# A gated-delta stage of a two-block kernel: loads, sums, masks and block turns reordered across its queues

## The chip, the cores and the metric

One core of one Trainium2 chip. The metric is the device time of the whole program in microseconds (us), median of several runs.

## What is computed

The program runs two model blocks on a 512-token latent and a 256-token context of width 2048. The change lies in one stage of the first block, the gated-delta mixer (8 heads of width 128, two directions). Per head, with 6 chunks of 128 tokens:

```python
q = l2_norm(qkv[:, :, 0]) * (K ** -0.5); k = l2_norm(qkv[:, :, 1]); v = qkv[:, :, 2]
gcum = jnp.cumsum(g, axis=-1)
decay = jnp.exp(jnp.where(incl, gcum[..., :, None] - gcum[..., None, :], -jnp.inf))
a_strict = jnp.where(strict, jnp.einsum('bhcik,bhcjk->bhcij', k_beta, k) * decay, 0.0)
sol = lax.linalg.triangular_solve(a_strict, rhs, left_side=True, lower=True, unit_diagonal=True)
attn = jnp.einsum('bhcik,bhcjk->bhcij', q, k) * decay
q_dec = q * jnp.exp(gcum)[..., None]
def step(S, inp):
    qd, ke, ui, wi, ai, dec = inp
    v_new = ui - jnp.einsum('bhqk,bhkv->bhqv', wi, S)
    o = jnp.einsum('bhqk,bhkv->bhqv', qd, S) + jnp.einsum('bhqs,bhsv->bhqv', ai, v_new)
    return S * dec[..., None, None] + jnp.einsum('bhsk,bhsv->bhkv', ke, v_new), o
```

The first output normalisation, the output projection and the second block follow in other stages.

## The kernel before, in words

The stage is `gdn_stage`. Each engine has its own list of instructions, written out by hand, and waits on semaphores; the order within an engine's list is fixed. Heads are worked in four pairs (`PAIRS`, j = 0 to 3). In the opening, heads 0 to 3 are prepared, and 8 output columns of the output projection of the other mixer half (`mix`, matmuls of L2356 to L2358) run on TensorE beside VectorE's triangle of pair 0. Then the loop over pairs; `more` means that there is a next pair, `ahead` that there is one after it (true for j = 0 and 1), whose heads are a+2, b+2 in the lists (a, b inside `steps`).

Work of a pair, in the order of TensorE: `level5_t` (L476) needs the spread inverse blocks (`scatter_in`, the SyncE loads of L319); `turn_k(a)`, `level5_x` (L490), `level5_y` (L501), `q_sums` of the heads ahead (L414), `turn_k(b)`, `level6_t` (L509), `finish(j - 1)` (L607), `level6_y` (L520), `turn_v`, `weights` (L538), `k_sums` of the heads ahead (L405, L406), then `steps(j)`. In `steps`, six steps n = 0 to 5, each for two directions: L565, L570 and, after ScalarE's scaled copy `v_end` (L784), L578, which VectorE turns into the new state (L1091 for n = 0, L1095 after); from n = 2 on L598 and L599 write the outputs. Between the steps of pairs 0 and 1 stand the products of the heads ahead: `queries` (L451) and `products` (L461).

ScalarE takes the squares of q and k (`square_q` L696, `square_k` L688), logarithm and inverse root (`ln_*`, `inverse_*` L715, L711), the evacuations, the exponentials of the decay (`decay`, L732, 12 small ones a head) and of q's scale (`queries`, L738), `turn_tri` (L742), and the norm of the pair before (`norm_ln` L838, `norm_exp` L842). VectorE scales k (`keys`, L1030), evacuates (`level5_x`, L1053), solves the 32-wide triangles of the next pair (`triangle`, L1043 and L1046, 31 of them, `TRI_EARLY` of them ahead of `steps`), ends the pair before (`finish`, L1111, L1113), normalises q (`norm_q`, L1005) and k (L1000), makes `attention` (L1010), `decayed` (L1017) and `turned` (L1024). GpSimd adds the mask to the decay's argument (`argument`, L952), multiplies q with its scale (`queries`, L957), writes the identity (`identity`, L964) and issues stores. SyncE issues the loads; `gather` (L287, 8 transfers a head) writes the Gram parts to memory, `blocks_load` (L294) reads them back as 32-wide blocks, `scatter_out` (L299) and `scatter_in` (L319) move the solved blocks.

## Time and profile before

| What | us |
|---|---|
| Median of 3 runs (3778.26 to 3779.26) | 3778.9 |
| The profiled execution | 3775.26 |
| its span, first to last instruction | 3773.5 |
| the gated-delta stage in it, 972 to 1384 us | 412 |

Mean granted clock of TensorE is 0.975 over the span. Times in the rows below are us from the start of the span; a line of a timeline has start, duration, engine, source line, and in brackets how long the engine was idle before it and who ended that.

### The profile page before, as it was taken

What the parts mean: (1) busy time and instruction counts of PE and PEld (TensorE: products, weight loads), DVE (VectorE), ACT (ScalarE), POOL (GpSimd) and SP (SyncE); (2) the same over time, 40 slices, a digit from 0 to 9 for tenths busy, and PEclk for the clock granted to TensorE, in tenths of its full rate; (3) what the DMA queues carried; (4) which work ended last, traced back from release to release, by engine and by line L of the source; (5) the groups of instructions that cost most, each with busy time, mean ns of one, the idle gap of its engine ahead of it and who ended that gap; (6) DMA issues with size and microseconds to landing.
All of it is one profiled execution on the core that took longest, in us unless ns stands there. A gap on an engine that the chain in (4) does not pass through costs nothing. (4 is left out here: it accounts for less than half of the span.)

```text
span 3773.5 us, 49646 instructions
## 1 busy us (share of the span) xinstructions
PE 3565.7 (94%) x19794; PEld 2959.4 (78%) x19794; DVE 1966.6 (52%) x2979; ACT 1510.6 (40%) x2532; POOL 471.2 (12%) x362
## 2 busy tenths in 40 slices
PE   6999999899776789999999999999999999999998
PEld 4688888787655668888888788888888888888886
DVE  7455555467566634755455553436533444454543
ACT  3322222254644443565565642324222444442332
POOL 1000000134211000011011160120000000025021
PEclk8999999999988899999999999999999999999999
DMA  9734323332533336422223163335634555543332
GB/s 360 260 131 137 114 95 103 96 98 59 180 107 92 97 119 195 126 84 87 86 74 93 54 201 98 95 90 103 132 115 124 123 94 111 111 128 101 93 95 89
DMA packets 580503, 448.37 MB, mean 119 GB/s; under 512 B 64454, under 2 KB 500114, under 8 KB 579504
## 3 DMA queue, kind: packets, MB, share of 16 engines
q1 hardware_dynamic: 572080, 421.18, 39.6%
q10 hardware_dynamic: 6048, 19.14, 1.3%
q0 software_dynamic: 2144, 4.87, 0.4%
q8 instruction: 157, 2.57, 0.3%
q14 instruction: 74, 0.61, 0.1%
HBM read 387.61 MB, written 57.46 MB: 118 GB/s over the span
## 5 line engine op out<-in xcount | busy, mean ns | idle before, releaser
L2379 DVE TENSOR_TENSOR w_lo<-w,w_hi 128x512 fp32r<-128x512 f32 x429 | 291.3, 698 | 500.1 <-ACT w_hi L2372 499.9
L2372 ACT ACTIVATE w_hi<-w 128x512 fp32r<-128x512 f32 x429 | 260.9, 625 | 478.0 <-PE od_acc L2358 171.1
L4511 DVE TENSOR_TENSOR w_lo<-w,w_hi 128x512 fp32r<-128x512 f32 x260 | 232.2, 899 | 353.6 <-ACT w_hi L4404 352.2
L4370 PE MATMUL ta_acc<-u_hi,w_hi 128*128 128x512 f32 x960 | 375.2, 391 | 2.8 <-POOL u_lo L4305 1.4
L4372 PE MATMUL ta_acc<-u_hi,w_lo 128*128 128x512 f32 x960 | 373.6, 389 | 0.0
L4371 PE MATMUL ta_acc<-u_lo,w_hi 128*128 128x512 f32 x960 | 373.5, 389 | 0.0
L4404 ACT ACTIVATE w_hi<-w 128x512 fp32r<-128x512 f32 x260 | 163.5, 630 | 440.8 <-PE ta_acc L4372 433.9
L2356 PE MATMUL od_acc<-u_hi,w_hi 128*128 128x512 f32 x768 | 304.7, 397 | 0.0
L2358 PE MATMUL od_acc<-u_hi,w_lo 128*128 128x512 f32 x768 | 299.3, 390 | 0.0
L2357 PE MATMUL od_acc<-u_lo,w_hi 128*128 128x512 f32 x768 | 299.0, 389 | 0.0
L2356 PE MATMUL ev_acc<-u_hi,w_hi 128*128 128x512 f32 x608 | 250.3, 412 | 14.7 <-DVE w_lo L2379 5.1
L2358 PE MATMUL ev_acc<-u_hi,w_lo 128*128 128x512 f32 x608 | 238.8, 393 | 0.0
L2357 PE MATMUL ev_acc<-u_lo,w_hi 128*128 128x512 f32 x608 | 238.7, 393 | 0.0
L1941 PE MATMUL p_acc<-u_hi,p_w_hi 128*128 128x512 f32 x544 | 215.8, 397 | 2.9 <-DVE p_w_lo L1749 2.5
L1948 PE MATMUL p_acc<-u_hi,p_w_lo 128*128 128x512 f32 x544 | 216.0, 397 | 0.0
L4370 PEld LDWEIGHTS ta_acc<-u_hi,w_hi 128*128 128x128 f32 x960 | 180.2, 188 | 43.7 <-DVE u_lo L4519 3.1
L1942 PE MATMUL p_acc<-u_lo,p_w_hi 128*128 128x512 f32 x544 | 212.2, 390 | 0.0
L4372 PEld LDWEIGHTS ta_acc<-u_hi,w_lo 128*128 128x128 f32 x960 | 180.2, 188 | 37.6
L4371 PEld LDWEIGHTS ta_acc<-u_lo,w_hi 128*128 128x128 f32 x960 | 180.2, 188 | 37.5 <-issue 0.5
L2085 DVE TENSOR_TENSOR p_w_lo<-p_w,p_w_hi 128x1024 fp32r<-128x1024 f32 x66 | 80.4, 1223 | 225.1 <-ACT p_w_hi L1987 225.1
L1987 ACT ACTIVATE p_w_hi<-p_w 128x1024 fp32r<-128x1024 f32 x66 | 69.6, 1060 | 247.9 <-PE p_acc L1948 178.0
L2357 PEld LDWEIGHTS od_acc<-u_lo,w_hi 128*128 128x128 f32 x768 | 144.3, 188 | 31.0 <-issue 1.9
(754 smaller groups left out, 8062.4 us busy)
## 6 DMA issues: line engine op xcount, KB each, us to landing
w<-in_o_w_in_dram SPq DMA_DIRECT2D x260, 256.0 KB, 6.6
w<-in_e_w_in_dram SPq DMA_DIRECT2D x144, 256.0 KB, 2.9
p_w<-in_w_in_dram SPq DMA_DIRECT2D x70, 512.0 KB, 6.2
mod_w<-in_w_ada_dram SPq DMA_DIRECT2D x32, 1024.0 KB, 11.8
w<-in_ple_gate_w_dram SPq DMA_DIRECT2D x128, 256.0 KB, 2.7
gate_w<-in_w_ada_dram SPq DMA_DIRECT2D x16, 1024.0 KB, 5.7
z_w<-in_w_in_dram SPq DMA_DIRECT2D x64, 256.0 KB, 2.9
w<-in_e_w_out_dram SPq DMA_DIRECT2D x64, 256.0 KB, 2.7
```

The source lines that it names most:

```text
L1941: pe.matmul(lat, wh, x_hi[:, k, :], start=first, stop=False)
L1942: pe.matmul(lat, wh, x_lo[:, k, :], start=False, stop=False)
L1948: last = pe.matmul(lat, wl, x_hi[:, k, :], start=False, stop=end)
L2356: pe.matmul(out, hi, self.x_hi[:, k, :], start=first, stop=False)
L2357: pe.matmul(out, hi, self.x_lo[:, k, :], start=False, stop=False)
L2358: last = pe.matmul(out, lo, self.x_hi[:, k, :], start=False, stop=end)
L2372: act.activation(self.w_hi[m % self.ring][:], self.w[m % self.ring][:], ACT.Copy).then_inc(self.hi_set, 1)
L2379: eng.tensor_tensor(self.w_lo[m % self.ring][:], self.w[m % self.ring][:], self.w_hi[m % self.ring][:].bitcast(F32), ALU.subtract).then_in ...
L4370: pe.matmul(bank, hi, hi_x[:, k, :], start=(k == 0), stop=False)
L4371: pe.matmul(bank, hi, lo_x[:, k, :], start=False, stop=False)
L4372: last = pe.matmul(bank, lo, hi_x[:, k, :], start=False, stop=(k == job.kd - 1))
L4511: dve.tensor_tensor(self.w_lo[m % RING][:], self.w[m % RING][:], self.w_hi[m % RING][:].bitcast(F32), ALU.subtract).then_inc(self.lo_set, 1)
```

## The change

Nothing of the arithmetic changes; instructions are moved.

- GpSimd's eight mask additions (`argument`) and eight q scalings (`queries`) become VectorE's: in the opening for heads 0 to 3 and 0 to 1, in the loop the scalings after the early triangles, the mask additions in step 0 of `steps`.
- `TRI_EARLY` goes from 14 to 18, ten instead of six triangle steps stand ahead of `finish`.
- SyncE: `scatter_in(0)` ahead of `gather(2)`; `load_q` of the heads ahead goes in front of `blocks_load`.
- TensorE: `q_sums` after `level6_t`; `finish` after `turn_v(a)`; `k_sums` from ahead of `steps` to its step n = 1; `queries` and `products` one step later, the last part after `steps`.
- ScalarE: squares and logarithm of q, `norm_ln`, `norm_exp` later, squares of k ahead of the scalings' exponentials, decay exponentials a step later, `turn_tri` at n = 3 instead of 4.
- VectorE: norms of k, `attention`, `decayed`, `turned` half a step to a step later; `decayed(b, 1)` after the steps.

```diff
--- before.py
+++ after.py
@@ -203,7 +203,7 @@
         S_STEPS = 2 * (CHUNKS - 1)
         O_STEPS = 2 * LC
         TRI_STEPS = B32 - 1
-        TRI_EARLY = 14
+        TRI_EARLY = 18
         MIX_SOLVED = 56
 
         def by_job(upto, eng, step):
@@ -343,8 +343,8 @@
                 load_v(hd)
             mix.load_weights(sp, len(mix.chunks))
             scatter_out(0)
+            scatter_in(0)
             gather(2)
-            scatter_in(0)
             gather(3)
             sp.wait_ge(mix.chunk_done, len(mix.chunks))
             mix.wait_stored(sp)
@@ -352,13 +352,13 @@
             for j in range(PAIRS):
                 more, ahead = j + 1 < PAIRS, j + 2 < PAIRS
                 a, b = 2 * j + 4, 2 * j + 5
+                if ahead:
+                    load_q(a)
+                    load_q(b)
                 if more:
                     blocks_load(j + 1)
                 if not more:
                     tail.load_weights(sp, len(tail.chunks))
-                if ahead:
-                    load_q(a)
-                    load_q(b)
                 if more:
                     load_qdec(2 * j + 2)
                     load_qdec(2 * j + 3)
@@ -547,16 +547,17 @@
                 pe.wait_ge(k_copied, 4 * (j + 1))
                 for n in range(CHUNKS):
                     if ahead:
-                        if n == 2:
+                        if n == 1:
+                            k_sums(a)
+                            k_sums(b)
+                        if n == 3:
                             queries(a)
                             products(a, range(0, 4))
-                        if n == 3:
+                        if n == 4:
                             products(a, range(4, CHUNKS))
-                        if n == 4:
+                        if n == 5:
                             queries(b)
                             products(b, range(0, 4))
-                        if n == 5:
-                            products(b, range(4, CHUNKS))
                     if not more and n in (2, 4):
                         tail.pe_steps(pe, TAIL)
                     for d in range(2):
@@ -641,31 +642,30 @@
                     tail.pe_steps(pe, TAIL)
                 level5_x(j)
                 level5_y(j)
-                if ahead:
-                    q_sums(a + 2)
-                    q_sums(b + 2)
                 if more:
                     turn_k(b)
                 else:
                     tail.pe_steps(pe, TAIL)
                 level6_t(j, 0)
                 level6_t(j, 1)
-                if j > 0:
-                    finish(j - 1)
+                if ahead:
+                    q_sums(a + 2)
+                    q_sums(b + 2)
                 level6_y(j, 0)
                 level6_y(j, 1)
                 if more:
                     turn_v(a)
                 else:
                     tail.pe_steps(pe, TAIL)
+                if j > 0:
+                    finish(j - 1)
                 weights(j, 0)
                 if more:
                     turn_v(b)
                 weights(j, 1)
+                steps(j)
                 if ahead:
-                    k_sums(a + 2)
-                    k_sums(b + 2)
-                steps(j)
+                    products(b + 2, range(4, CHUNKS))
                 if more and not ahead:
                     pe.wait_ge(v_copied, 2 * GDN_H)
                     pe.wait_ge(k_copied, 2 * GDN_H)
@@ -792,11 +792,10 @@
                         if n == 0:
                             ln_k(a)
                             inverse_k(a)
-                            decay(a, range(0, 3))
                         if n == 1:
                             ln_k(b)
                             inverse_k(b)
-                            decay(a, range(3, 6))
+                            decay(a, range(0, 2))
                     for d in range(2):
                         c = ORDER[d][n]
                         if 2 <= n < 4:
@@ -810,10 +809,10 @@
                                            ACT.Copy).then_inc(o_set, 1)
                     if ahead:
                         if n == 2:
-                            decay(b, range(0, 3))
-                        if n == 3:
-                            decay(b, range(3, 6))
-                    if j + 1 < PAIRS and n == 4:
+                            decay(a, range(2, 6))
+                        if n == 4:
+                            decay(b, range(0, 6))
+                    if j + 1 < PAIRS and n == 3:
                         turn_tri(j + 1)
                     if j == PAIRS - 2 and n >= 2:
                         k = n - 2
@@ -900,21 +899,19 @@
                     copy_k(a)
                 else:
                     tail_job(2)
-                if ahead:
-                    square_q(a + 2)
-                    square_q(b + 2)
                 level5_y(j)
                 if more:
                     copy_k(b)
                 else:
                     tail_job(3)
                 if ahead:
+                    square_q(a + 2)
+                    square_q(b + 2)
+                level6_t(j, 0)
+                level6_t(j, 1)
+                if ahead:
                     ln_q(a + 2)
                     ln_q(b + 2)
-                level6_t(j, 0)
-                level6_t(j, 1)
-                if j > 0:
-                    norm_ln(j - 1)
                 level6_y(j, 0)
                 level6_y(j, 1)
                 if more:
@@ -922,20 +919,22 @@
                 else:
                     tail_job(4)
                 if j > 0:
-                    norm_exp(j - 1)
+                    norm_ln(j - 1)
                 weights(j, 0)
                 if more:
                     copy_v(b)
+                if j > 0:
+                    norm_exp(j - 1)
                 weights(j, 1)
                 if ahead:
-                    inverse_q(a + 2)
-                    inverse_q(b + 2)
+                    square_k(a + 2)
+                    square_k(b + 2)
                 if more:
                     queries(a)
                     queries(b)
                 if ahead:
-                    square_k(a + 2)
-                    square_k(b + 2)
+                    inverse_q(a + 2)
+                    inverse_q(b + 2)
                 steps(j)
                 square(j)
                 if more and not ahead:
@@ -947,16 +946,6 @@
 
         @block.gpsimd
         def _(pool):
-            def argument(hd):
-                pool.wait_ge(arg_in[hd % 4], 16 * (hd // 4 + 1))
-                pool.tensor_tensor(a_t[hd % 4][:], a_t[hd % 4][:], neg[:].unsqueeze(1).to_broadcast([P, CHUNKS, 2, P]), ALU.add).then_inc(dec_arg, 1)
-
-            def queries(hd):
-                pool.wait_ge(q_normed, hd + 1)
-                pool.wait_ge(qdec_exp, hd + 1)
-                pool.tensor_tensor(qdec[hd % 4][:], qdec[hd % 4][:], q_n[hd % 4].rearrange("p (c q) -> p c q", c=LC).unsqueeze(2)
-                                   .to_broadcast([P, LC, 2, P]), ALU.mult).then_inc(q_decayed, 1)
-
             def identity(j):
                 if j > 0:
                     for n in range(2):
@@ -965,21 +954,12 @@
                 pool.wait_ge(tri_init, 2 * j + 1)
                 pool.memset(tri[:].rearrange("p i j -> p (i j)")[:, 0:B32 * B32:B32 + 1], 1.0).then_inc(tri_init, 1)
 
-            for hd in range(4):
-                argument(hd)
             identity(0)
-            queries(0)
-            queries(1)
             for n in range(MIX_JOBS):
                 mix.store(pool, n)
             for j in range(PAIRS):
                 if j + 1 < PAIRS:
                     identity(j + 1)
-                    queries(2 * j + 2)
-                    queries(2 * j + 3)
-                if j + 2 < PAIRS:
-                    argument(2 * j + 4)
-                    argument(2 * j + 5)
             for n in range(len(tail.jobs)):
                 tail.store(pool, n)
 
@@ -1003,6 +983,16 @@
                 dve.wait_ge(q_inv, hd + 1)
                 dve.wait_ge(q_squared, hd + 1)
                 dve.tensor_tensor(q_n[hd % 4], q_n[hd % 4], sq_q[hd % 2][:], ALU.mult).then_inc(q_normed, 1)
+
+            def argument(hd):
+                dve.wait_ge(arg_in[hd % 4], 16 * (hd // 4 + 1))
+                dve.tensor_tensor(a_t[hd % 4][:], a_t[hd % 4][:], neg[:].unsqueeze(1).to_broadcast([P, CHUNKS, 2, P]), ALU.add).then_inc(dec_arg, 1)
+
+            def queries(hd):
+                dve.wait_ge(q_normed, hd + 1)
+                dve.wait_ge(qdec_exp, hd + 1)
+                dve.tensor_tensor(qdec[hd % 4][:], qdec[hd % 4][:], q_n[hd % 4].rearrange("p (c q) -> p c q", c=LC).unsqueeze(2)
+                                  .to_broadcast([P, LC, 2, P]), ALU.mult).then_inc(q_decayed, 1)
 
             def attention(hd):
                 dve.wait_ge(dec_set, hd + 1)
@@ -1066,20 +1056,26 @@
                                     triangle(j + 1, at)
                                     at += 1
                             if ahead and slot == 1:
+                                if n == 0 and d == 0:
+                                    argument(a)
                                 if n == 0 and d == 1:
+                                    argument(b)
+                                if n == 1 and d == 1:
                                     norm_k(a)
-                                if n == 1 and d == 1:
+                                if n == 2 and d == 0:
                                     norm_k(b)
-                                if n == 2 and d == 1:
+                                if n == 3 and d == 0:
                                     attention(a)
-                                if n == 3:
-                                    decayed(a, d)
+                                if n == 3 and d == 1:
+                                    decayed(a, 0)
                                 if n == 4 and d == 0:
+                                    decayed(a, 1)
+                                if n == 4 and d == 1:
                                     turned(a)
-                                if n == 4 and d == 1:
+                                if n == 5 and d == 0:
                                     attention(b)
-                                if n == 5:
-                                    decayed(b, d)
+                                if n == 5 and d == 1:
+                                    decayed(b, 0)
                             if slot == 0 and n < CHUNKS - 1:
                                 dve.wait_ge(s_ready, S_STEPS * j + 2 * n + d + 1)
                                 if n >= 2:
@@ -1102,6 +1098,7 @@
                             dve.tensor_tensor(o[:, :, cols], o[:, :, cols], bank[6 + d][:, 0:256].rearrange("p (h q) -> p h q", h=2),
                                               ALU.add).then_inc(o_set, 1)
                 if ahead:
+                    decayed(b, 1)
                     turned(b)
 
             def finish(j):
@@ -1118,6 +1115,8 @@
                     dve.tensor_tensor(y_lo[:, k, :], y_lo[:, k, :].bitcast(F32), y_hi[:, k, :].bitcast(F32), ALU.subtract
                                       ).then_inc(mix.x_set, 1)
 
+            for hd in range(2):
+                argument(hd)
             for hd in range(2):
                 norm_k(hd)
             for hd in range(2):
@@ -1131,6 +1130,10 @@
             mix.split_low(dve, 1)
             split_y(range(2, MIX))
             mix.split_low(dve, mix.ring)
+            for hd in range(2, 4):
+                argument(hd)
+            for hd in range(2):
+                queries(hd)
             for n in range(TRI_STEPS):
                 triangle(0, n)
                 if n in (7, 9):
@@ -1157,14 +1160,17 @@
                     dve.memset(y_by_d[1][:], 0.0).then_inc(cleared, 1)
                 if not more:
                     tail.split_low(dve, 6)
-                for n in range(6 if more else 0):
+                for n in range(10 if more else 0):
                     triangle(j + 1, n)
                 if j > 0:
                     finish(j - 1)
                 if not more:
                     tail.split_low(dve, len(tail.chunks))
-                for n in range(6, TRI_EARLY if more else 0):
+                for n in range(10, TRI_EARLY if more else 0):
                     triangle(j + 1, n)
+                if more:
+                    queries(2 * j + 2)
+                    queries(2 * j + 3)
                 if ahead:
                     norm_q(2 * j + 4)
                     norm_q(2 * j + 5)
```

## Rows read from the trace of the kernel before

**Rows 1.** Stretches of the stage: us, busy of each engine, TensorE's granted clock, transfers

```profile
972.00:1073.40 101.40, 77.23 (x372) 61.12 (x372) 78.71 (x119) 57.60 (x121) 27.39 (x18) 0.89 0.57 176
1073.40:1156.85 83.45, 57.13 (x701) 50.02 (x701) 48.61 (x106) 42.22 (x99) 12.83 (x6) 0.82 0.34 92
1156.85:1247.10 90.25, 60.25 (x705) 51.20 (x705) 55.06 (x108) 44.34 (x102) 13.15 (x6) 0.81 0.33 91
1247.10:1317.60 70.50, 53.87 (x680) 47.34 (x680) 46.81 (x106) 33.28 (x73) 5.41 (x3) 0.86 0.41 106
```

**Rows 2.** Waits from 970 to 1384 us: who waited for whom, us, times, longest

```profile
PE gdn_bank L570 <- DVE gdn_state L1091: 17.5, 3, 6.9
...
PE gdn_bank L414 <- ACT kq L696: 12.9, 2, 7.0
...
PE gdn_bank L405 <- ACT gdn_sq_k L688: 12.9, 5, 4.5
```

**Rows 3.** Stretches, same columns (PE, PEld, DVE, ACT, POOL): triangles alone, then beside GpSimd

```profile
1085.50:1095.80 10.30, 8.21 (x115) 5.96 (x116) 9.25 (x28) 7.40 (x16) 0.00 (x0) 0.80 0.63 216
...
1190.40:1202.60 12.20, 7.06 (x28) 4.76 (x28) 12.06 (x5) 7.01 (x16) 12.04 (x4) 0.85 0.20 76
1269.60:1274.60 5.00, 1.85 (x14) 1.48 (x12) 4.93 (x3) 1.89 (x5) 4.83 (x2) 1.00 0.95 289
```

**Rows 4.** Groups of instructions, GpSimd, 970 to 1384 us: count, busy us, mean ns, idle before

```profile
L952 POOL TENSOR_TENSOR gdn_a_t<-gdn_a_t,k_neg 128x1536 f32<-128x1536 f32 x8 | 29.6, 3724 | 41.7 <-DMA gdn_a_t<-s_cum_rows 41.7
L957 POOL TENSOR_TENSOR gdn_qdec<-gdn_qdec,kq 128x1024 f32<-128x1024 f32 x4 | 10.2, 2568 | 68.8 <-ACT gdn_qdec L738 68.8
```

**Rows 5.** Groups of instructions, VectorE, 1050 to 1390 us

```profile
L1030 DVE TENSOR_TENSOR gdn_w_neg<-gdn_k_tok,gdn_tabs 128x1536 f32<-128x1536 f32 x8 | 13.6, 1736 | 0.0
...
L1010 DVE TENSOR_TENSOR gdn_attn<-gdn_bank,gdn_a_t 128x1024 f32<-128x1024 f32 x6 | 7.3, 1210 | 0.0
...
L1005 DVE TENSOR_TENSOR kq<-kq,gdn_sq_q 128x512 f32<-128x512 f32 x1 | 0.7, 692 | 0.0
```

**Rows 6.** Timeline of pair 0, from the last weights to the gather of the fifth head

```profile
1101.70 0.60 ACT L771 ACTIVATE gdn_w_neg<-gdn_bank 128x512 f32<-128x512 f32 x1 [0.30 <-PE gdn_bank L538]
...
1105.31 1.56 ACT L688 ACTIVATE gdn_sq_k<-kq 128x768 f32<-128x768 f32 x2
...
1112.64 0.49 DVE L1091 COPY gdn_state<-gdn_bank 128x128 f32<-128x128 f32 x2 [7.62 <-PE gdn_bank L578]
...
1113.05 3.57 DVE L1043 TENSOR_TENSOR gdn_part<-gdn_blk,gdn_tri 96x256 f32<-96x256 f32 x1
...
1132.65 0.71 PE L461 MATMUL gdn_bank<-kq 128*128 128x128 f32 x4 [3.20 <-DVE gdn_attn L1010]
...
1147.89 2.12 SPq L287 DMA_DIRECT2D s_blocks_in<-gdn_a_t  x4
```

**Rows 7.** Timeline of pair 1, from its first product to its first state copy

```profile
1156.85 1.02 PE L476 MATMUL gdn_bank<-gdn_x_m,gdn_a_t 32*32 32x32 f32 x96 [3.34 <-DMA gdn_x_m<-s_blocks_out]
...
1168.61 0.20 DVE L1043 TENSOR_TENSOR gdn_part<-gdn_blk,gdn_tri 96x31 f32<-96x31 f32 x1 [4.56 <-DMA gdn_blk<-s_blocks_in]
...
1183.93 0.69 DVE L1111 TENSOR_TENSOR gdn_o<-gdn_o,gdn_o_sq 128x512 f32<-128x512 f32 x1 [11.85 <-ACT gdn_o_sq L842]
...
1205.71 0.49 DVE L1091 COPY gdn_state<-gdn_bank 128x128 f32<-128x128 f32 x2
```

**Rows 8.** Timeline of the opening: norms, then the moves of solved blocks

```profile
993.18 2.05 PE L451 MATMUL gdn_bank<-kq 128*128 128x128 f32 x8 [8.34 <-DVE kq L1005]
...
1064.40 2.12 SPq L287 DMA_DIRECT2D s_blocks_in<-gdn_a_t  x4
...
1073.44 1.50 PE L476 MATMUL gdn_bank<-gdn_x_m,gdn_a_t 32*32 32x32 f32 x96 [7.11 <-issue]
```

**Rows 9.** Timeline of pair 2: first triangle step, first state copy

```profile
1258.08 0.20 DVE L1043 TENSOR_TENSOR gdn_part<-gdn_blk,gdn_tri 96x31 f32<-96x31 f32 x1 [4.70 <-DMA gdn_blk<-s_blocks_in]
...
1278.78 0.49 DVE L1091 COPY gdn_state<-gdn_bank 128x128 f32<-128x128 f32 x2
```

## The prediction

> **What bounds the kernel now.** I read the stretches first. In the four of the gated-delta stage TensorE is busy for 57 to 60 of 83 to 90 us in pairs 0 and 1, 54 of 70.5 in pair 2, and the granted clock falls to 0.81 to 0.89 [rows 1]. No engine fills its time: the stage is a chain that goes from engine to engine, and what counts is which wait ends last at each hand-over. The table of waits names three of TensorE's: for the first state copy of VectorE (17.5 us in 3), for the squares of q (12.9 in 2) and for the squares of k (12.9 in 5) [rows 2]. Then I asked why VectorE is late with the first state copy. In the third view, 14 triangle steps (28 instructions) take 10.3 us when GpSimd is idle. From 1190.4 to 1202.6 VectorE finishes five instructions in 12.06 busy us while GpSimd is busy for 12.04; in pair 2 three take 4.93 beside GpSimd's 4.83 [rows 3]. In pair 0 a triangle product takes 3.57 us beside GpSimd's mask addition [rows 6]. A GpSimd operation here takes 3.7 us (mask) or 2.6 us (q scaling) [rows 4], and each VectorE instruction that meets one lasts until it is over. So the stall is in front of the state copy, on the path.
>
> **The parts and their prices**, as time gained up to fixed points: the first state copy of each pair (L1091), and the first product of the next (L476).
>
> *GpSimd's 16 operations to VectorE.* The nearest rows in VectorE are 1.74 us for two operands of 128x1536 in SBUF, one broadcast, and 1.21 us for a 128x1024 product [rows 5]. Eight and eight make 23.5 us of new VectorE work. What it removes: in pair 1 12.06 us for five instructions that alone take 0.37 each (10.3 over 28), 10.2 us; in pair 2 4.93 less 1.1, 3.8 us; in pair 0 3.57 less 0.4, 3.2 us [rows 3, 6]. The bounds of one moved mask addition are 1.2 and 3.7 us, I take 1.74, the same shape.
>
> *Opening and pair 0 up to its state copy.* TensorE's 8.34 us for the norms shrink [rows 8], but ScalarE then waits in its own list for a load and comes about as before; I keep 3.5 us at the end of the mix. Solved blocks issued ahead of `gather(2)` come 2.1 to 4.3 us earlier (a gather is two lines of 2.12) [rows 8], but the third and fourth head's Gram parts that much later, so the triangles of pair 1 start about 1 us later. The terms: last weight evacuation at 1102.3 [rows 6]; it comes 3 us earlier, since squares of q, fetched ahead of the blocks, no longer stand before the fifth level: 1099.3. Behind it ScalarE has squares of k, exponentials and inverse roots, 4.6 us (1102.3 to 1106.87) [rows 6], say 5.0: 1104.3. VectorE: two q norms at 0.69 [rows 5] and one triangle of 0.9: state copy at 1106.6 instead of 1112.64, **6.0 us gained**. TensorE's wait for squares of k (4.5 the longest) [rows 2] goes with it: `k_sums` run while it would wait for VectorE anyway. What is late next is VectorE: 18 triangles (10.3 plus four of 0.9 = 13.9 us) and two scalings of 1.2 end at about 1103 to 1104. Bounds: 3 us, were the load of q not earlier; 8, if the opening keeps its gain.
>
> *Steps of pair 0.* Before, 35.25 us from state copy (1112.64) to `gather(a)` (1147.89) [rows 6]. After: VectorE bounds n = 0 to 2 with 13 triangle steps (about 9), two mask additions (3.5), norms of k (1.9) and states (3): 17.1 us. At n = 3 TensorE's 2.0 us of queries and products no longer wait for `attention` (3.20 before) [rows 6]; n = 3 and 4 cost 5.5 each, and `turn_tri`, now at n = 3, adds 1.0 to the scaled copies of n = 4. `turned(a)` ends at 28.9: **6.3 us gained**. `turned(a)` one slot later is in this. The gather, spread and first product behind it keep their 8.96 us (1147.89 to 1156.85) [rows 6, 7]. Bounds 3 and 7.
>
> *Pair 1 up to its state copy.* Before, 48.9 us (1156.85 to 1205.71) [rows 7]. After, on VectorE: triangles start 11.8 us after the first product as now (1168.61), ten take 6.7; then `finish` waits for `norm_exp`. Before it stood at 27.1 us (1183.93, an idle of 11.85) [rows 7]; TensorE's 7.0 us wait for q's squares [rows 2] goes, as its load no longer waits for the gathers, but `norm_exp` itself is moved behind two evacuations and a copy: 23.2. Then 2.9 for `finish`, 7.0 for eight triangles, 2.4 scalings, 1.4 norms, 0.9: 37.8. **11.1 us gained.** In parts: 10.2 of stall removed, 3.9 from the earlier norm, 3.6 spent on four triangles more and 2.4 on scalings, the rest is idle time filled. Bounds: 4.5, if the norm comes no earlier; 14, if it never waits.
>
> *Steps of pair 1.* As in pair 0 but without a GpSimd stall in them: 6.3 less 3.2, **3.1 us gained**. Bounds 0 and 5.
>
> *Pair 2.* Before, 20.7 us from triangle start to state copy [rows 9]. After: ten triangles 6.7, `finish` after a later `norm_exp` 2.5 + 2.9, eight 7.0, scalings 2.4, one 0.9: 22.4. **1.7 us lost**: the stall of 3.8 goes, but 3.6 of triangles and 2.4 of scalings stand in front, and the norm is later. Bounds 1 gained, 4 lost. In its steps ScalarE's `turn_tri` (2.0 us) at n = 3 lands before the scaled copies of n = 4, and smaller triangles give 1.0 back; in pair 3 the later `norm_exp` costs up to 0.7: together **1.5 lost**, bounds 0 and 3.
>
> *Costed at nothing:* `store_o`, `load_z`, `load_arg` (SyncE idles for long in the steps; without that cover about 1 us), and GpSimd's remaining stores.
>
> **Sum:** 6.0 + 6.3 + 11.1 + 3.1 - 1.7 - 1.5 = 23.3 us. The profiled execution took 3775.3, its span 3773.5; the median of the runs is 3778.9, 3.6 above it. I set the difference against the median: **3755.6 us**. All low ends add to 3.5 us gained, all high ones to 35.
>
> **Rivals.**
>
> A. *VectorE takes over.* Every wait that the new order removes on TensorE and ScalarE comes back as a wait for VectorE ahead of its first state copy, since four more triangles (3.6) and scalings (2.4) stand there in three pairs and two mask additions (3.5) in two: 25 us of work. Gained would be the stalls (10.2 + 3.8 + 3.2), the step-3 waits (3.2 twice) and half the opening: about 25. Net nothing: 3778. For it speaks that VectorE is already the late one in pairs 1 and 2 [rows 2]; against it, that it idles 11.85 us in pair 1 and 7.62 in pair 0, where the new work fits [rows 6, 7]. 12 %.
> The Trainium skill, Perfetto Trace Analysis, section Optimizing Scalar/DVE Operations, advises the opposite of this edit: when VectorE is saturated, give work to ScalarE or even GpSimd; by that rule this rival would come out. It adds that GpSimd and VectorE share a read port, so that such a move may not help. The stretch at 1190.4 agrees with the second sentence: 12.06 us for five instructions.
>
> B. *Slower.* The mechanism is the queue on VectorE in pairs 0 and 1: mask additions of step 0 stand before the second direction's state, and each holds that state 1.74 us or, if the shape is as dear there as on GpSimd, 3.7; four of them at 3.7 and six scalings at 2.6 in front of states are 30 us against 17.2 of stalls removed, and what else is gained (about 5) does not pay. That gives 3787. It decides from 3.0 us for a mask addition on. The 1.74 row speaks against. 4 %.
>
> C. *The loads of q come no earlier.* They share the transfer engines with the four block gathers; then the 7.0 and 5.9 us waits for squares stay in part, and pair 1 gains 6 instead of 11, pair 0 3: 3764. 18 %.
>
> **How the numbers follow.** My own sum has 66 %. About 0.2 % (7.6 us) is what a measurement of this kernel can tell from no change. The sum and C are beyond it; of the sum's low end (under 7.6 us gained) a small part is not. Faster 0.84, same 0.12, slower 0.04. The range holds the sum with most of its bounds and C, and stops short of A: 3745 to 3772.
>
> **What would show each step.** No VectorE triangle over 0.5 us between 972 and 1384; L952 and L957's work on VectorE at 1.7 and 1.2 us; TensorE's waits for L688 and L696 near nothing; a wait for L1091 still there, in pair 1 and 2; the stage's last store some 23 us earlier and all later stages of the same length. Wrong would be: the mask addition above 3 us, TensorE's wait for L1091 above 25 us, or the granted clock not recovering.

## The result and the profile after the change

The changed kernel takes 3745.95 us (median of 4 runs, 3743.34 to 3748.91), the kernel before, run beside it, 3778.58 (4 runs, 3773.43 to 3779.26). The ratio is 0.9915, with a 95 % interval from 0.990 to 0.993. That is 32.6 us less, where 23.3 were forecast; it lies in the range (3745 to 3772), within 1 us of its fast end. The profiled execution took 3745.8 us, its span is 3744.0, so in the two profiled executions the difference is 29.5 us.

The first view is the table of stretches, cut at the prediction's fixed points: the stage's start, the first product of each pair, the first state copy of each pair, the stage's end. The columns are those of [rows 1] (us, busy of TensorE, its weight loads, VectorE, ScalarE, GpSimd, then TensorE's granted clock, share and GB/s of the transfers). The kernel after:

```profile
971.43:1067.14 95.71, 76.19 (x372) 61.00 (x373) 69.04 (x122) 57.40 (x121) 6.55 (x12) 0.90 0.60 185
1067.14:1104.60 37.46, 25.03 (x477) 20.40 (x478) 25.93 (x50) 20.10 (x39) 0.00 (x0) 0.77 0.56 168
1104.60:1140.08 35.48, 29.12 (x224) 26.28 (x222) 26.83 (x61) 22.04 (x60) 1.11 (x2) 0.98 0.22 45
1140.08:1175.64 35.56, 28.57 (x492) 22.65 (x492) 24.44 (x52) 24.10 (x45) 0.00 (x0) 0.82 0.60 187
1175.64:1211.40 35.76, 27.61 (x212) 25.84 (x212) 27.09 (x61) 20.18 (x57) 1.11 (x2) 0.95 0.23 45
1211.40:1244.68 33.28, 21.69 (x480) 19.06 (x480) 22.98 (x51) 17.00 (x34) 0.00 (x0) 0.86 0.52 143
1244.68:1285.30 40.62, 32.82 (x196) 29.31 (x196) 22.40 (x58) 16.16 (x39) 0.54 (x1) 0.83 0.29 66
971.43:1352.46 381.03, 301.37 (x3194) 257.16 (x3195) 236.30 (x492) 207.22 (x463) 13.09 (x24) 0.90 0.41 119
```

The kernel before, its two stretches of steps in which heads ahead are prepared, and the whole stage:

```profile
1112.64:1156.85 44.21, 30.98 (x221) 29.15 (x220) 31.26 (x68) 21.95 (x60) 4.79 (x4) 0.88 0.18 36
1205.71:1247.10 41.39, 30.82 (x213) 28.86 (x213) 27.27 (x67) 18.82 (x51) 1.10 (x2) 0.87 0.19 38
972.43:1384.51 412.08, 308.75 (x3194) 262.07 (x3194) 246.87 (x476) 207.55 (x463) 62.55 (x40) 0.87 0.38 110
```

The stage is 31.05 us shorter (412.08 to 381.03); what follows it is 2.5 us longer in this pair of executions (2389.0 to 2391.5). Code that is the same in all kernels of this study, before and after the stage, moved by up to 4 us from one profiled execution to another, so the experiments are compared by the stage. Each stage is that of one profiled execution; the changed kernel was not run again beside the experiments, and the kernel before, which was, had medians from 3776.20 to 3779.25. Totals of two experiments are therefore best compared by their ratios.

The same fixed points in all kernels; the stage's end is the start of the next stage's first product. The opening is from the stage's start to the first product of pair 0, "to copy" from a pair's first product to its first state copy, "steps" from there to the next pair's first product. Each number is the length of a stretch of that kernel's own table.

| kernel | opening | pair 0 to copy | steps | pair 1 to copy | steps | pair 2 to copy | steps | pair 3 | stage |
|---|---|---|---|---|---|---|---|---|---|
| before | 101.0 | 39.2 | 44.2 | 48.9 | 41.4 | 31.7 | 38.8 | 66.9 | 412.1 |
| after | 95.7 | 37.5 | 35.5 | 35.6 | 35.8 | 33.3 | 40.6 | 67.2 | 381.0 |
| operations moved only | 97.4 | 41.2 | 45.1 | 41.1 | 45.7 | 29.8 | 37.5 | 67.2 | 404.9 |
| order only | 99.7 | 46.5 | 33.2 | 43.7 | 33.9 | 35.3 | 39.2 | 67.2 | 398.7 |
| after, scalings on GpSimd | 94.6 | 39.3 | 35.6 | 37.3 | 35.7 | 35.3 | 39.9 | 67.0 | 384.6 |
| after, load order of before | 98.3 | 31.8 | 35.9 | 42.3 | 35.9 | 33.2 | 40.1 | 67.2 | 384.7 |
| after, scatter alone put back | 97.3 | 30.6 | 36.7 | 34.8 | 36.1 | 35.0 | 40.1 | 67.5 | 378.1 |
| after, products at their old steps | 95.1 | 38.3 | 38.1 | 34.5 | 38.4 | 32.3 | 40.7 | 67.1 | 384.5 |
| after, 14 early triangles | 95.4 | 37.3 | 36.8 | 35.3 | 37.0 | 33.5 | 39.6 | 67.2 | 382.1 |
| after, late turn in pair 2 | 95.7 | 36.7 | 35.7 | 35.7 | 37.3 | 34.0 | 36.5 | 67.1 | 378.7 |
| after, light pair 2 | 95.3 | 37.3 | 35.6 | 35.1 | 35.9 | 25.1 | 41.4 | 67.3 | 372.9 |
| scatter back and light pair 2 | 98.3 | 31.1 | 35.5 | 34.9 | 36.4 | 25.1 | 40.1 | 67.3 | 368.7 |
| both, 14 early | 98.0 | 30.2 | 36.8 | 32.1 | 37.3 | 25.8 | 41.7 | 67.1 | 368.9 |
| both, 10 early | 95.7 | 29.8 | 38.6 | 29.8 | 39.4 | 25.4 | 40.0 | 67.1 | 365.9 |

How far a row can be trusted is seen in the steps of pair 1 in kernels that don't differ there: 35.8, 35.9, 36.1, 36.4, 37.3. A difference under about 1.5 us in one cell says nothing by itself.

The groups of instructions of the kernel after, VectorE in the stage, to be read beside [rows 4, 5]:

```profile
L989 DVE TENSOR_TENSOR gdn_a_t<-gdn_a_t,k_neg 128x1536 f32<-128x1536 f32 x8 | 13.9, 1750 | 0.7 <-DMA gdn_a_t<-s_cum_rows 0.7
L994 DVE TENSOR_TENSOR gdn_qdec<-gdn_qdec,kq 128x1024 f32<-128x1024 f32 x4 | 4.7, 1220 | 3.0 <-ACT gdn_qdec L738 3.0
L1036 DVE TENSOR_TENSOR gdn_tri<-gdn_tri,gdn_part 96x256 f32<-96x256 f32 x4 | 1.7, 421 | 0.1
```

The mask addition costs 1.75 us (1.74 was taken), the scaling 1.22 (1.21), and the widest triangle instruction 0.42 on average. And yet VectorE's busy time in the stage falls, from 246.87 to 236.30 us, with 16 instructions more. GpSimd's falls from 62.55 to 13.09. The 23.3 us of work that VectorE took over are less than the time it had stood still beside GpSimd.

The table of waits over the stage, the kernel after, to be read beside [rows 2]:

```profile
PE gdn_bank L571 <- DVE gdn_state L1087: 11.7, 3, 8.0
...
PE gdn_bank L418 <- DVE gdn_a_t L1007: 10.2, 2, 9.6
...
PE gdn_bank L405 <- ACT gdn_sq_k L688: 2.3, 2, 1.8
...
PE gdn_bank L414 <- ACT kq L696: 1.7, 2, 1.3
```

TensorE's waits for the squares, 12.9 us each before, are down to 2.3 and 1.7. The wait for the first state copies is 11.7 instead of 17.5, and 8.0 of it lie in pair 2 (6.6 before), where the stretch to the copy became longer. One wait has grown from 2.4 us to 9.6 at its longest: that for `decayed` in the opening.

### The profile page after: what moved, and what is told of

Its sections match the earlier page's. It is cut to its first block and busy times, and to the rows that moved or that the text cites. A ratio compares the mean times of both kernels' runs of the same rounds, so it can differ in the third digit from the quotient of the medians.

```text
span 3744.0 us, 49646 instructions
## 1 busy us (share of the span) xinstructions
PE 3561.0 (95%) x19794; PEld 2954.2 (79%) x19794; DVE 1957.4 (52%) x2995; ACT 1511.1 (40%) x2532; POOL 421.9 (11%) x346
## 5 line engine op out<-in xcount | busy, mean ns | idle before, releaser
L2362 PEld LDWEIGHTS od_acc<-u_hi,w_hi 128*128 128x128 f32 x768 | 144.3, 188 | 30.9 <-issue 1.9
```

What stands on the lines that cost most here:

```text
L2362: pe.matmul(out, hi, self.x_hi[:, k, :], start=first, stop=False)
```

## The experiments

**The two halves of the change.** First the kernel before with only the sixteen operations moved, its order otherwise kept. The cut shows the two instructions; their calls move to VectorE's list too, the scalings behind the early triangles, the mask additions into step 0:

```diff
-                pool.tensor_tensor(a_t[hd % 4][:], ...
+                dve.tensor_tensor(a_t[hd % 4][:], ...
-                pool.tensor_tensor(qdec[hd % 4][:], ...
+                dve.tensor_tensor(qdec[hd % 4][:], ...
```

> The kernel before with only GpSimd's 16 operations moved to VectorE; order, loads and the 14 early triangles as before. My theory (the stall beside GpSimd is on the path): from the first product of pair 1 to its first state copy 48.9 us become about 41 (10.2 of stall gone, 2.4 of scalings added), pair 2's 31.7 become about 30.3, the opening and pair 0 gain 5; the whole about 3762, 16 us below before. Rival A (VectorE's new work eats what the stalls give): the whole within 3 us of before, 3776 to 3779, and the waits for the first state copies as long as before.

Measured: 3767.84 us, ratio 0.9974 (0.9962 to 0.9986) against the kernel before at 3779.25; stage 404.9 us, 7.2 less. Rival A is refuted by the total. The stretches to the copy of pairs 1 and 2 came as the theory had them (41.1 and 29.8 us), but the opening and pair 0 gave 1.6 us instead of 5, and the steps of pair 1 took 45.7 us instead of 41.4, which nobody had on the list: the two mask additions now stand on VectorE there.

Then the changed kernel with those operations back on GpSimd, everything else as changed:

```diff
-                dve.tensor_tensor(a_t[hd % 4][:], ...
+                pool.tensor_tensor(a_t[hd % 4][:], ...
-                dve.tensor_tensor(qdec[hd % 4][:], ...
+                pool.tensor_tensor(qdec[hd % 4][:], ...
```

> The changed kernel with the 16 operations back on GpSimd, all the new order kept. My theory: the stalls come back, about 4 us in pair 0, 8 in pair 1, 2 to 4 in pair 2 and 5 in the opening, so about 3763, with triangle instructions of 2.4 to 3.6 us in the trace. Rival (order alone makes the gain, the long VectorE instructions were off the path): 3746 as the changed kernel.

Measured: 3763.35 us, ratio 0.9959 (0.9945 to 0.9973); stage 398.7 us, 13.4 less. The total is the theory's, in part by luck: pair 0 pays 9.0 us to its copy instead of 4, and the steps of pairs 0 and 1 give 4.2 back. Together they would be 20.6 by addition; the whole change gives 31.05. By the stages the two halves help each other by about 10 us, by the medians (11.4 and 15.9 of 32.6) by 5, which is no more than an interval of either; the profiled execution of the first half took 3772.45 us, 4.6 above its median, so its stage may be too long. That they help each other is better seen in the stretches. The timelines say how. The order-only kernel, GpSimd, then VectorE in the same stretch of pair 1 (its triangles are L1042 and L1045):

```profile
1178.90 4.83 POOL L956 TENSOR_TENSOR gdn_qdec<-gdn_qdec,kq 128x1024 f32<-128x1024 f32 x2 [33.88 <-ACT gdn_qdec L738]
1183.69 7.16 POOL L951 TENSOR_TENSOR gdn_a_t<-gdn_a_t,k_neg 128x1536 f32<-128x1536 f32 x2
```

```profile
1178.56 0.41 DVE L1042 TENSOR_TENSOR gdn_part<-gdn_blk,gdn_tri 96x240 f32<-96x240 f32 x1
1179.00 2.52 DVE L1045 TENSOR_TENSOR gdn_tri<-gdn_tri,gdn_part 96x240 f32<-96x240 f32 x1
1181.55 2.45 DVE L1042 TENSOR_TENSOR gdn_part<-gdn_blk,gdn_tri 96x247 f32<-96x247 f32 x1
1184.04 3.53 DVE L1045 TENSOR_TENSOR gdn_tri<-gdn_tri,gdn_part 96x247 f32<-96x247 f32 x1
1187.61 3.52 DVE L1042 TENSOR_TENSOR gdn_part<-gdn_blk,gdn_tri 96x252 f32<-96x252 f32 x1
1191.16 0.42 DVE L1045 TENSOR_TENSOR gdn_tri<-gdn_tri,gdn_part 96x252 f32<-96x252 f32 x1
```

Four GpSimd operations, four VectorE instructions that last as long as each of them, then 0.42 us again. The Trainium skill, SBUF — State Buffer, section Who interferes with whom, states that a VectorE instruction with two inputs in SBUF contends with a GpSimd instruction that reads SBUF; these rows agree, 2.45 to 3.53 us against 0.41. In pair 0 of the same kernel the two mask additions last 8.36 us instead of 7.16, and in that time VectorE runs two q norms of 0.68 us each unstretched. It looks as if the waiting goes both ways; no run was made to test it.

In the old order such a stall cost nothing in pair 0, for VectorE idled 7.62 us ahead of the copy [rows 6]: moving the operations made that stretch no shorter there (39.2 to 41.2). In the new order VectorE is the late one in all three pairs, four triangles more stand ahead of the copy, and GpSimd's operations cost 9.0, 8.1 and 2.0 us there (46.5, 43.7, 35.3 against 37.5, 35.6, 33.3).

**Which of the two kinds of operation.**

```diff
             def queries(hd):
-                dve.tensor_tensor(qdec[hd % 4][:], ...
+                pool.tensor_tensor(qdec[hd % 4][:], ...
```

> The changed kernel with only the eight scalings of q back on GpSimd, the mask additions staying on VectorE. Theory, VectorE stands still for the length of each GpSimd operation: two scalings are 4.8 to 5.1 us of GpSimd in a pair (in the order-only kernel), against 2.35 us of VectorE's own, so each first stretch of pairs 0 to 2 gets 2.5 us longer and the steps, which keep the masks, stay: total 7 to 8 us above the changed kernel, 3753. Rival: it is the mask additions, 7.2 to 8.4 us a pair of GpSimd, that do all the harm (they lie right behind the scalings in the queue); then the total is within 2 us of the changed kernel.

Measured: 3749.91 us (ratio 0.9926, 0.9911 to 0.9941), stage 384.6, 3.6 above the changed kernel. The three stretches to the copy are longer by 1.9, 1.7 and 2.0 us and the steps are not: the place is the theory's, the size is between theory and rival. Its VectorE rows show why (its triangles are L1037 and L1040):

```profile
1167.91 2.52 DVE L1040 TENSOR_TENSOR gdn_tri<-gdn_tri,gdn_part 96x240 f32<-96x240 f32 x1
1170.46 2.45 DVE L1037 TENSOR_TENSOR gdn_part<-gdn_blk,gdn_tri 96x247 f32<-96x247 f32 x1
1172.95 0.41 DVE L1040 TENSOR_TENSOR gdn_tri<-gdn_tri,gdn_part 96x247 f32<-96x247 f32 x1
```

The held instructions are not lost, each gets its own 0.41 us of work done. So two scalings cost 4.97 - 0.82 = 4.15 us of standing still and save 2.35 of work: 1.8 net. That is about what all three pairs show. For two mask additions the same sum is 7.16 - 0.84 = 6.3 us in pair 1, and from this kernel to the order-only one its stretch grows by 6.4 (37.3 to 43.7); pair 2, which has no mask addition, is 35.3 in both. In return the steps of pairs 0 and 1, without the mask additions on VectorE, are 2.4 and 1.8 us shorter. The four of the opening are worth 5.1 us there (94.6 to 99.7). The mask additions are thus some 14 of the 17.7 us between the order-only kernel and the changed one, the scalings 3.6.

**The loads.** The changed kernel with SyncE's order of before:

```diff
-            scatter_in(0)
             gather(2)
+            scatter_in(0)
             gather(3)
...
-                if ahead:
-                    load_q(a)
-                    load_q(b)
                 if more:
                     blocks_load(j + 1)
...
+                if ahead:
+                    load_q(a)
+                    load_q(b)
```

> The changed kernel with SyncE's order of before: gather of the third head ahead of the spread of pair 0, loads of q behind the load of the blocks. My theory: pair 1 loses about 3 us from its first product to its state copy only if the squares of q bound it; the first product of pair 0 comes 3 to 4 us later; the whole 3749 to 3754. Rival (VectorE's triangles bound pair 1, q's load is covered): pair 1 unchanged, the whole within 2 us of 3746.

Measured: 3749.05 us (ratio 0.992, 0.9905 to 0.9935), stage 384.7. The theory's place is right and its size too small: the early loads of q are worth 6.7 us in pair 1 (42.3 to 35.6), not 3. The first product of pair 0 comes 2.6 us later, where 3 to 4 were expected. This kernel's VectorE shows the finish waiting 9.46 us for the norm of the pair before, as in [rows 7]; the changed kernel waits 1.39:

```profile
1169.41 0.69 DVE L1108 TENSOR_TENSOR gdn_o<-gdn_o,gdn_o_sq 128x512 f32<-128x512 f32 x1 [9.46 <-ACT gdn_o_sq L841]
```

```profile
1161.46 0.69 DVE L1108 TENSOR_TENSOR gdn_o<-gdn_o,gdn_o_sq 128x512 f32<-128x512 f32 x1 [1.39 <-ACT gdn_o_sq L841]
```

But from the stage's start to the first copy it is 3.1 us faster than the changed kernel (130.1 against 133.2). One of SyncE's two edits helps and the other hurts. So the scatter alone went back behind `gather(2)`:

```diff
-            scatter_in(0)
             gather(2)
+            scatter_in(0)
             gather(3)
```

> The changed kernel with one line moved: the first block scatter of a pair is issued behind gather(2) again, while the loads of q stay where the change put them. Theory: the opening's and pair 0's way to the first state copy (133.2 us after the change, 130.1 with the whole load order of before) is long because the gathers stand behind that scatter; it becomes about 130, pair 1's way to the copy stays at 35.6 (not 42.3 as with the loads of before), total about 3743. Rival: q's loads themselves, sitting ahead of the others, cost the 3 us; then the first stretch stays at 133 and the total at 3746.

Measured: 3740.3 us (ratio 0.9904, 0.9889 to 0.9919), stage 378.1. Start to first copy is 127.9 us, 5.3 less than with the change, and pair 1 takes 34.8. That is the theory's outcome, by more than it said. The ratio's interval overlaps the changed kernel's, so the gain is read from this stretch: it is 132.4 to 133.9 us in the changed kernel and the five variants that keep its scatter and its mask additions, and 125.6 to 130.1 in the five that have the scatter behind `gather(2)`. VectorE's `turned` of the fourth head, the changed kernel first, then this one:

```profile
1073.13 0.98 DVE L1014 STREAM_TRANSPOSE gdn_a_turned<-gdn_a_t 128x768 f32<-128x768 f32 x1 [11.61 <-DMA s_blocks_in<-gdn_a_turned]
```

```profile
1069.33 0.98 DVE L1014 STREAM_TRANSPOSE gdn_a_turned<-gdn_a_t 128x768 f32<-128x768 f32 x1 [4.44 <-DMA s_blocks_in<-gdn_a_turned]
```

The turned blocks of that head overwrite a buffer that `gather(2)` has to read first. With the scatter ahead of the gather, VectorE stands for 11.61 us, and `keys`, the evacuations and the next pair's triangles are queued behind it. Counted from the stage's start, the scatter ahead brings the first product 1.6 us earlier (95.7 and 97.3) and the first copy 5.3 us later. The same line moved in the kernel with the light pair 2 (below) is worth less: 3.2 us to the first copy (132.6 to 129.5), 4.2 of stage.

**The products' steps.** The changed kernel with sums, products and what follows them at their old places:

```diff
-                        if n == 1:
-                            k_sums(a)
-                            k_sums(b)
-                        if n == 3:
+                        if n == 2:
                             queries(a)
                             products(a, range(0, 4))
```

(the second head's parts, the exponentials and `attention`, `decayed`, `turned` likewise.)

> The changed kernel with the sums of k ahead of the steps and queries, products, decay exponentials, norms, attention, decayed and turned at their slots of before. My theory (the removed waits for attention in step 3 and for squares of k make the step gain): from state copy to next first product pairs 0 and 1 take 39 to 41 us instead of 35.5 and 35.8, and the squares of k hold TensorE about 3 us more in pair 0; the whole 3754 to 3758. Rival (the steps got shorter because VectorE had fewer triangles and no GpSimd beside it): 36 to 37 us each, the whole 3747 to 3749.

Measured: 3749.61 us (ratio 0.9922, 0.9907 to 0.9936), stage 384.5. Both preparing stretches of steps are 2.6 us longer (38.1 and 38.4), between the 39 to 41 of the theory and the 36 to 37 of its rival, whose total it nearly is. The squares of k, which were to hold TensorE about 3 us more in pair 0, don't: its stretch to the copy is 38.3 us against 37.5. So the products' places are part of what shortened the steps, and not the whole. What a wait cost in the steps of before is best seen in TensorE's timeline. The kernel before, pair 1:

```profile
1222.17 0.75 PE L461 MATMUL gdn_bank<-kq 128*128 128x128 f32 x4 [3.35 <-DVE gdn_attn L1010]
1222.72 1.06 PE L565 MATMUL gdn_bank<-gdn_v_tok,gdn_y_m 128*128 128x128 f32 x4
1223.58 1.06 PE L570 MATMUL gdn_bank<-gdn_state,gdn_w_neg 128*128 128x128 f32 x4
1224.43 1.06 PE L565 MATMUL gdn_bank<-gdn_v_tok,gdn_y_m 128*128 128x128 f32 x4
1225.28 1.02 PE L570 MATMUL gdn_bank<-gdn_state,gdn_w_neg 128*128 128x128 f32 x4
```

The kernel after, the same five groups:

```profile
1195.80 0.61 PE L461 MATMUL gdn_bank<-kq 128*128 128x128 f32 x4
1196.25 0.61 PE L566 MATMUL gdn_bank<-gdn_v_tok,gdn_y_m 128*128 128x128 f32 x4
1196.69 0.61 PE L571 MATMUL gdn_bank<-gdn_state,gdn_w_neg 128*128 128x128 f32 x4
1197.14 0.61 PE L566 MATMUL gdn_bank<-gdn_v_tok,gdn_y_m 128*128 128x128 f32 x4
1197.59 0.61 PE L571 MATMUL gdn_bank<-gdn_state,gdn_w_neg 128*128 128x128 f32 x4
```

The wait of 3.35 us has gone, and so has what stood behind it. Before, the granted clock is 1.00 ahead of the wait and 0.52 from 1222.72 to 1226.30, the lower level (1.2 GHz), then 1.00 again; after, it is 1.00 throughout, the higher level (2.4 GHz). From the first group's start to the fifth's end it is 4.1 us before and 2.4 after, 1.7 more. The 3.20 us of pair 0 look the same (0.53 from 1134.2 to 1137.6), and so do the waits for state copies (3.97 us, then 0.52; 6.87, then 0.50); waits of 1.27 us at 1148.42 and 1238.18 are followed by groups at the full pace of 0.45. Over the whole stretch of steps the granted clock is 0.98 and 0.95 after the change, 0.88 and 0.87 before, 0.91 and 0.87 in the kernel with the products at their old steps. In pair 1 TensorE is busy for 30.82 us before and 27.61 after with the same 212 or 213 matmuls. The clock isn't always on the path: with the scalings on GpSimd it is 1.00 and 0.90 in the two stretches, and they last 35.6 and 35.7.

**The triangles.** The changed kernel with four early triangles fewer:

```diff
-        TRI_EARLY = 18
+        TRI_EARLY = 14
...
-                for n in range(10 if more else 0):
+                for n in range(6 if more else 0):
                     triangle(j + 1, n)
```

> The changed kernel with 14 early triangles a pair in place of 18 (6 ahead of the state copies, 8 behind). Theory 1, the first stretch of a pair is set by what VectorE has to do before the state copies: pairs 1 and 2 reach the copy 4 triangles' work (0.6 to 0.9 us each) sooner, 35.6 and 33.3 us become about 33 and 31, and the steps, 35.5 and 35.8 us, stay within 1 us, since TensorE's chain sets them; total about 3741. Theory 2, VectorE is what bounds the steps too: the work only moves, steps 38 to 39 us, total within 2 us of the changed kernel.

Measured: 3747.35 us (ratio 0.9919, 0.9904 to 0.9934), stage 382.1. The total is theory 2's, but the steps grow by only 1.3 and 1.2 us, in each cell no more than the noise, less than it said and a little more than theory 1 allowed, and the stretch to the copy doesn't shrink (35.3, 33.5) as theory 1 wanted. The two are not told apart, by a fault of the edit. It took the four triangles from ahead of `finish`, where VectorE has idle time: in pair 2 the finish now waits 6.45 us for the norm instead of 1.88, and the same eight triangles and the scalings stand behind it.

**Pair 2.** Two edits where the change itself lost time. First the turn alone:

```diff
-                    if j + 1 < PAIRS and n == 3:
+                    if j + 1 < PAIRS and n == (3 if ahead else 4):
                         turn_tri(j + 1)
```

> The changed kernel, but the blocks of the last pair but one are turned at the fifth step again, as before the change (pairs 0 and 1 still at the fourth). Theory, that the turn and its transposes at the fourth step lengthen pair 2's steps: 40.6 us becomes about 38.6, total about 3744. Rival: the 1.8 us that pair 2's steps lost come from the products' wait for decays one step later; then no difference.

Measured: 3741.8 us (ratio 0.9907, 0.9893 to 0.9922), stage 378.7. Pair 2's steps are 36.5 us instead of 40.6, twice the 2 us expected; the rival is refuted. The wait for the scaled copy behind the turn is 1.75 us of the 4.1; TensorE's busy time in the stretch falls by another 1.9 (32.82 to 30.94, granted clock 0.83 to 0.87). TensorE's timeline, the changed kernel first, then this one:

```profile
1264.29 1.22 PE L579 MATMUL gdn_bank<-gdn_v_end,gdn_k_tok 128*128 128x128 f32 x8 [1.99 <-ACT gdn_v_end L784]
```

```profile
1266.66 1.23 PE L579 MATMUL gdn_bank<-gdn_v_end,gdn_k_tok 128*128 128x128 f32 x8 [0.24 <-ACT gdn_v_end L784]
```

Then also fewer triangles ahead of the copy (`early` is 10 in pair 2 and 18 in pairs 0 and 1), and the last pair's scalings inside the steps. The cut leaves out the lines that put the triangles and scalings there:

```diff
-                for n in range(10, TRI_EARLY if more else 0):
+                for n in range(min(10, early), early):
                     triangle(j + 1, n)
-                if more:
+                if ahead:
                     queries(2 * j + 2)
                     queries(2 * j + 3)
```

> The changed kernel with three edits for the last pair but one: its blocks turned at the fifth step, only 10 triangles of the last pair early (the other 8 in the steps), and the last pair's q scaled inside the second step and not ahead of the state copies. If the copy of pair 2 waits for VectorE's work ahead of it, 33.3 us become 26 to 28, the steps grow from 40.6 by less than that (to about 42), total about 3741. Rival: the steps take all of it back, or the last pair (25.7 us to its copy) waits for the scaled q; total 3746 or more.

Measured: 3738.12 us (ratio 0.99, 0.9884 to 0.9917), stage 372.9. The copy of pair 2 comes after 25.1 us instead of 33.3 (26 to 28 were expected), and it waits for TensorE, no longer the other way round:

```profile
1235.93 0.49 DVE L1089 COPY gdn_state<-gdn_bank 128x128 f32<-128x128 f32 x2 [1.03 <-PE gdn_bank L579]
```

The steps carry eight triangles more and are 41.4 us, 4.9 over the kernel with the late turn alone; of 8.9 us gained ahead of the copy 4.0 stay.

**Together.** Scatter back, and pair 2 light:

> Two edits together: the first block scatter behind gather(2), and the lighter pair 2 (turn at the fifth step, 10 early triangles, q's scaling in the second step). If they act on different stretches they add: 381.0 - 2.9 - 8.1 = 370 us of stage, total about 3735. Rival: what pair 2 loses ahead of its copy grows with an earlier start (35.0 us there with the scatter alone, 33.3 without), and the two give less than the better alone plus 1; total 3738.

Measured: 3735.38 us (ratio 0.9887, 0.9872 to 0.9901), stage 368.7. They add, as expected: 12.3 us of stage against 11.0 by addition. The two variants on top of it change only the early triangles of pairs 0 and 1 (`TRI_EARLY` 14, then 10, those taken away being behind `finish`):

> The same as the kernel with both edits, and 14 early triangles for the pairs ahead, all 4 fewer of them behind the finish and not ahead of it as in the first trial with 14. The copy of pair 1 then comes 3.4 us sooner (8 products of 0.4 us) and the steps take 1.2 us longer each, as with 14 before: stage 4 us shorter over two pairs, total 3731. Rival: pair 1's steps are VectorE's by then and give it all back: total 3735.

> 10 early triangles for all pairs, none behind the finish. Theory, TensorE's state products bound the copy: with pair 1's product of ends done about 5.5 us ahead of the copy after the change, the copy comes at most 5.5 us sooner, of which 3.4 with 14; the steps pay 2.4 us for 8 more triangles. Total 3730, 1 us better than with 14. Rival: the steps pay 4 or more, since late triangles delay the norms of k behind them: total 3734 or above.

Measured: 3732.35 us (ratio 0.9877, 0.986 to 0.9893) and 3732.97 us (0.988, 0.9866 to 0.9895). The expected 3731 and 3730 were not reached, and the intervals overlap that of the kernel with both edits, so no gain from them is shown. By the stretches the triangles move: with 14 the copy of pair 1 comes 2.8 us sooner (3.4 were expected); with 10, the copy of pair 1 comes 5.1 us sooner and the steps of pairs 0 and 1 take 3.1 and 3.0 more. In that kernel VectorE's scalings wait 1.07 us for ScalarE's exponentials just ahead of the copy, so TensorE, against the expectation, is not yet what bounds it:

```profile
1164.93 2.36 DVE L994 TENSOR_TENSOR gdn_qdec<-gdn_qdec,kq 128x1024 f32<-128x1024 f32 x2 [1.07 <-ACT gdn_qdec L738]
```

All three are faster than both kernels of the case: some 43 to 46 us below the kernel before, 11 to 14 below the 3745.95 of the changed one. The intervals of the last two lie clear of the changed kernel's (0.990 to 0.993); that of the first just touches it.

## Why the prediction was right, and where its sizes were off

| Term | forecast | measured | after against before |
|---|---|---|---|
| opening and pair 0 to its copy | 6.0 | 7.0 | 140.2 to 133.2 |
| steps of pair 0 | 6.3 | 8.7 | 44.2 to 35.5 |
| pair 1 to its copy | 11.1 | 13.3 | 48.9 to 35.6 |
| steps of pair 1 | 3.1 | 5.6 | 41.4 to 35.8 |
| pair 2 to its copy | -1.7 | -1.6 | 31.7 to 33.3 |
| its steps and pair 3 | -1.5 | -2.1 | 105.7 to 107.8 |

The direction and the signs of all terms held, and each lies inside its bounds or (steps of pairs 0 and 1, by 1.7 and 0.6 us) past them. Every gain came out larger than forecast, 31.05 us of stage and 32.6 of the median for 23.3, so the total met the range with 1 us to spare. The signs named ahead are there: no triangle above 0.5 us, 1.75 and 1.22 us for the moved operations, the waits for squares nearly gone, a wait for the first copy left (in pair 1 1.4 us of 6.9, and 2.4 for the other direction's).

**The stall** was priced rightly at 10.2 us in pair 1, and undoing it there costs 8.1 net of the work taken over (10.2 less 2.4 of scalings was forecast). The price of a mask addition, 1.74 us with the end 3.7 kept for the range, decided against rival B and measured 1.75.

**The opening** came as forecast, and for the reason given. The 8.34 us for the norms [rows 8] go with GpSimd's mask additions: with the moved operations alone 0.27 is left, with the order alone 8.42. ScalarE then waits in its own list for a load, 5.75 us where it had waited 5.81, VectorE waits for ScalarE's exponentials, and TensorE for `decayed` behind them. The kernel after:

```profile
991.15 1.15 ACT L846 ACTIVATE mx_y_hi<-mx_y_lo 128x512 fp32r<-128x512 f32 x2 [5.75 <-DMA mx_y_lo<-s_y]
...
995.83 1.23 DVE L1000 TENSOR_TENSOR gdn_attn<-gdn_bank,gdn_a_t 128x1024 f32<-128x1024 f32 x1 [6.30 <-ACT gdn_a_t L732]
...
999.06 1.51 PE L418 MATMUL gdn_bank<-k_ident,kq 128*128 128x128 f32 x6 [9.55 <-DVE gdn_a_t L1007]
```

With the operations moved alone the opening is 3.6 us shorter (101.0 to 97.4); 3.5 were kept. What was wrong is the price of "solved blocks ahead of `gather(2)`": triangles of pair 1 about 1 us later. What was not followed is the buffer that `gather(2)` frees for VectorE's `turned`. Against the same kernel with the scatter behind, the price up to the copy is 5.3 us, or 3.2 in the other pair of kernels that differ by it alone.

**Pair 1** forecast `finish` at 23.2 us after the first product; it came at 21.4 (1140.08 to 1161.46), which is 1.8 of the 2.2 us by which the copy was earlier than forecast.

**The steps** are the term that was mis-sized, by 2.4 and 2.5 us. Cut at the points that the prediction used, in us:

| From | to | forecast | pair 0, before and after | pair 1, before and after |
|---|---|---|---|---|
| first copy | VectorE's last state of n = 2 | 17.1 | 17.9, 15.3 | 14.3, 15.3 |
| there | end of `turned(a)` | 11.8 | 15.5, 11.7 | 15.7, 11.7 |
| there | `gather(a)` | 0 | 1.9, 0.0 | 1.9, 0.0 |
| there | next first product | 8.96 | 9.0, 8.4 | 9.45, 8.7 |

VectorE bounds the first three steps, as forecast: it is never idle in them. But its work there was put at 17.1 us and took 15.3 in both pairs. The prediction counted thirteen triangle steps at about 9 us. One of the thirteen had been counted ahead of the copy already, and the twelve that are left are the narrow ones (0.40 down to 0.18 us an instruction), 7.5 us of busy time together. (Its four entries add to 17.4, not 17.1.) The rest of the surplus, 0.5 and 0.8 us, lies in the transfers. The second line came as forecast: the waits for `attention` (3.20 and 3.35 us) have gone, and with them the 3.4 to 3.6 us at half the clock behind each. The products' old steps give back 0.5 and 0.1 us of the first line and 1.9 of the second in both pairs.

The third line is a gain that the prediction counts in its 35.25 us without naming it. SyncE issues `gather(a)` behind `scatter_out`, and that waits for `turn_tri`. Before, ScalarE's turn (L742) ends 1.1 us after VectorE's `turned(a)` (L1024), and the gather follows at 1147.89 [rows 6]:

```profile
1145.01 2.04 ACT L742 ACTIVATE gdn_blk<-gdn_tri 96x1024 f32<-96x1024 f32 x1
1145.03 0.97 DVE L1024 STREAM_TRANSPOSE gdn_a_turned<-gdn_a_t 128x768 f32<-128x768 f32 x1
...
1147.08 0.77 SPq L299 DMA_DIRECT2D s_blocks_out<-gdn_blk  x2
```

After, the turn is out of the way one step ahead:

```profile
1125.23 1.99 ACT L742 ACTIVATE gdn_blk<-gdn_tri 96x1024 f32<-96x1024 f32 x1
...
1130.66 0.97 DVE L1014 STREAM_TRANSPOSE gdn_a_turned<-gdn_a_t 128x768 f32<-128x768 f32 x1
...
1131.66 1.77 SPq L287 DMA_DIRECT2D s_blocks_in<-gdn_a_t  x4
```

The prediction priced the earlier `turn_tri` as a cost of 1.0 us alone. It frees 1.9 us where a gather stands behind it, in pairs 0 and 1, and only costs in pair 2, where none does. No run had the late turn in pairs 0 and 1 of the new order, so the 1.9 is read from the two traces and not tested.

The moved operations don't shorten the steps. In the old order they lengthen them (44.2 to 45.1 and 41.4 to 45.7 us), in the new one too (33.2 to 35.5 and 33.9 to 35.8): the whole gain of the steps is the order's.

**Pair 2** lost what was forecast, and its causes are shown: fewer triangles and no scaling ahead of the copy bring it 8.9 us sooner, and the turn at the fourth step alone costs 4.1 us there, where 2.0 were taken and 1.0 returned for smaller triangles.

**The rivals.** A, that VectorE takes over and gives everything back, came true in pair 2 alone, where TensorE's wait for VectorE's copy grew from 6.6 to 8.0 us. In pairs 0 and 1 VectorE sets the copy too (with 10 early triangles that of pair 1 comes 5.1 us sooner), but what it takes there the steps don't have to do, and the idle time named against the rival held most of the new work. B named 3.0 us for a mask addition as its threshold, which doesn't follow from its own sum (with scalings at 2.6 us it would break even at about 1.7); both prices were measured lower, 1.75 and 1.22 us. What B describes is there in small: in pair 1 a mask addition stands ahead of the second direction's first state, and TensorE waits 2.4 us for it. C priced the late loads well and is refuted as a forecast: with the loads of before pair 1 takes 42.3 us (C had 42.9), and the changed kernel takes 35.6. The Trainium skill's advice to give work to GpSimd (Perfetto Trace Analysis, section Optimizing Scalar/DVE Operations) would have made this kernel slower, which that section itself allows for: the order-only kernel, which does that to the changed one, is 17.7 us of stage behind it.
